# Four-layer transformer block on one core: where the input tile of the third and fourth layer begins in SBUF

## The reference

```python
def first_block(x, ...):
    for layer in range(DEPTH):                    # 2
        h = rms_norm(x, g_mix[layer])
        x = x + (even_mixer if layer == 0 else odd_mixer)(h, ...)   # attention
        h = rms_norm(x, g_mlp[layer])
        x = x + squared_relu_mlp(h, w_up[layer], w_down[layer])     # 1024 -> 4096 -> 1024
...
def mlstm_mixer(h, w_in, ...):                    # third layer
    x_in, z = jnp.split(h @ w_in, 2, axis=-1)     # 1024 -> 4096
    ...
def nsa_mixer(h, w_in, ...):                      # fourth layer
    q, k_c, v_c, k_s, v_s, k_w, v_w, z, g_logit = jnp.split(h @ w_in, ..., axis=-1)
    ...
```

## Time and profile before

| | |
|---|---|
| median of 3 runs | 935.82 us (935.81 to 936.11) |
| time of the profiled execution | 935.42 us |
| its span | 933.6 us |
| mean granted TensorE clock | 0.998 of 2.4 GHz |
| TensorE busy | 921.1 us, 99% |
| LDWEIGHTS / VectorE / ScalarE busy | 84% / 67% / 60% |

### The profile page before, as it was taken

The page is one execution under the profiler, slowest core; times in us unless marked ns, Lnnn a source line. Parts: engine busy times, 40 slices in busy tenths (PEclk is TensorE's granted clock), DMA queues, the critical chain, the costliest instruction groups (busy, mean ns, idle before and its releaser), DMA issues.

```text
span 933.6 us, 14097 instructions
## 1 busy us (share of the span) xinstructions
PE 921.1 (99%) x5584; PEld 784.7 (84%) x5584; DVE 629.9 (67%) x1137; ACT 561.8 (60%) x927; POOL 100.5 (11%) x145
## 2 busy tenths in 40 slices
PE   9999999999999999999999999999999999999997
PEld 7876888888888877788888888999988889988876
DVE  6767687764455666568776354677479847777885
ACT  6697565553435687755554343656477547868773
POOL 0210000000000000000000007155002201311101
PEclk9999999999999999999999999999999999999999
DMA  9843565555554435146555565233333642731201
GB/s 365 317 138 125 181 214 191 180 193 208 185 181 161 156 133 178 64 142 220 201 188 185 199 212 209 92 135 136 136 135 101 232 176 98 258 126 53 99 23 46
DMA packets 23017, 153.51 MB, mean 164 GB/s; under 512 B 2632, under 2 KB 2888, under 8 KB 5544
## 3 DMA queue, kind: packets, MB, share of 16 engines
q1 hardware_dynamic: 22024, 149.17, 44.5%
q0 software_dynamic: 640, 3.15, 1.0%
q10 hardware_dynamic: 288, 0.30, 0.1%
HBM read 150.57 MB, written 1.05 MB: 162 GB/s over the span
## 4 chain that ended last, share of the span: by engine, by line
PE 89%; ACT 4%; DVE 4%; issue 1%; DMA 1%; SPq 0%; ACTq 0%; DVEq 0%
PE bank L189 19%; PE bank L190 18%; PE bank L191 18%; PE bank L1165 13%; PE bank L1169 7%; PE bank L931 1%; PE bank L2334 1%; PE bank L955 1%; PE bank L944 1%; PE bank L1607 1%; PE bank L2325 1%; PE bank L2349 1%; DVE w_hi_lo L159 1%; PE bank L761 1%; PE bank L1592 1%
## 5 line engine op out<-in xcount | busy, mean ns | idle before, releaser
L159 DVE TENSOR_TENSOR w_hi_lo<-raw,w_hi_lo 128x2048 fp32r<-128x2048 f32 x121 | 277.3, 2295 | 135.4 <-ACT w_hi_lo L155 135.3
L155 ACT ACTIVATE w_hi_lo<-raw 128x2048 fp32r<-128x2048 f32 x135 | 257.8, 1912 | 107.8 <-PE bank L191 106.3
L189 PE MATMUL bank<-h,w_hi_lo 128*128 128x256 f32 x448 | 128.3, 286 | 0.2 <-DVE ml_x L1869 0.2
L190 PE MATMUL bank<-h,w_hi_lo 128*128 128x256 f32 x448 | 124.7, 278 | 0.0
L191 PE MATMUL bank<-h,w_hi_lo 128*128 128x256 f32 x448 | 124.6, 278 | 0.0
L1165 PE MATMUL bank<-h,w_hi_lo 128*128 128x512 f32 x512 | 123.1, 391 | 0.0
L1165 PEld LDWEIGHTS bank<-h,w_hi_lo 128*128 128x128 f32 x512 | 93.8, 188 | 18.3 <-issue 0.2
L189 PE MATMUL bank<-w_hi_lo,mlp_u_hi 128*128 128x512 f32 x256 | 99.8, 390 | 0.0
L190 PE MATMUL bank<-w_hi_lo,mlp_u_hi 128*128 128x512 f32 x256 | 99.6, 389 | 0.0
L191 PE MATMUL bank<-w_hi_lo,mlp_u_lo 128*128 128x512 f32 x256 | 99.6, 389 | 0.0
L190 PEld LDWEIGHTS bank<-h,w_hi_lo 128*128 128x128 f32 x448 | 84.7, 189 | 0.4 <-issue 0.2
(11 more groups left out here) (400 smaller groups left out, 1578.9 us busy)
## 6 DMA issues: line engine op xcount, KB each, us to landing
raw<-in_chunks SPq DMA_DIRECT2D x136, 1024.0 KB, 4.8
even_bias<-in_even POOLq DMA_DIRECT2D x8, 384.0 KB, 3.4
xres<-in_x SPq DMA_DIRECT2D x2, 512.0 KB, 5.4
raw<-in_chunks SPq DMA_DIRECT2D x2, 512.0 KB, 6.4
ml_z<-in_ml SPq DMA_DIRECT2D x1, 896.0 KB, 6.5
nsa_qtwo<-nsa_qraw SPq DMA_DIRECT2D x8, 80.0 KB
small<-in_small SPq DMA_DIRECT2D x1, 559.5 KB, 11.9
final_gain<-in_fnorm SPq DMA_DIRECT2D x1, 512.0 KB, 3.4
```

What stands on the lines that cost most here:

```text
L155: act.activation(w_hi[slot][:, :], raw[slot][:, :], ACT.Copy).then_inc(hi_ready, 1)
L159: dve.tensor_tensor(w_lo[slot][:, :], raw[slot][:, :], w_hi[slot][:, :].bitcast(F32), ALU.subtract).then_inc(lo_ready, 1)
L189: pe.matmul(dst, a_hi, b_hi, start=start, stop=False)
L190: pe.matmul(dst, a_hi, b_lo, start=False, stop=False)
```

## The change

The room of `h` begins 32 bytes earlier (the pad in front of it is 24 floats in place of 32) and has 8 floats more, so that everything behind it stays where it was. Within it there are now three views. `h` of the first two layers is 24 floats in, at its old address (residue 128). `h_ml` of the third layer is 16 floats in: residue 96, 32 bytes below the weights. `h_nsa` of the fourth is at the start: residue 32, 96 bytes below. Names are replaced accordingly, the writers of the tile (`Turned`) included. No instruction is added, removed or moved on any engine.

```diff
-    sb(ctx, "pad_h", [P, 32])
+    sb(ctx, "pad_h", [P, 24])
...
-    H_SHIFT = 16
+    H_SHIFT, ML_SHIFT, NSA_SHIFT = 24, 16, 0
     h_room = sb(big, "h", [P, H_SHIFT + KT * 2 * S], F32R)
-    h_moved = h_room[:, 0:KT * 2 * S].rearrange("p (k x s) -> p k x s", k=KT, x=2)
-    h = h_room[:, H_SHIFT:H_SHIFT + KT * 2 * S].rearrange("p (k x s) -> p k x s", k=KT, x=2)
+    h, h_ml, h_nsa = (h_room[:, at:at + KT * 2 * S].rearrange("p (k x s) -> p k x s", k=KT, x=2)
+                      for at in (H_SHIFT, ML_SHIFT, NSA_SHIFT))
...
-                last = product(pe, dst, w_hi[slot][:, cols], w_lo[slot][:, cols], hm_hi[:, k, :], hm_lo[:, k, :],
+                last = product(pe, dst, w_hi[slot][:, cols], w_lo[slot][:, cols], h_ml[:, k, 0, :], h_ml[:, k, 1, :],
...
-    ml_turned = Turned("mlin", sm("ml_norm"), (4, 5, 6, 7), h_moved)
+    ml_turned = Turned("mlin", sm("ml_norm"), (4, 5, 6, 7), h_ml)
...
-                last = product(pe, dst, w_hi[slot][:, cols], w_lo[slot][:, cols], hm_hi[:, k, :], hm_lo[:, k, :],
+                last = product(pe, dst, w_hi[slot][:, cols], w_lo[slot][:, cols], h_nsa[:, k, 0, :], h_nsa[:, k, 1, :],
...
-            last = wide_half(pe, c, t, bank[2 + t][:, :], hm_hi, hm_lo, range(part * WIDE_KT, (part + 1) * WIDE_KT),
+            last = wide_half(pe, c, t, bank[2 + t][:, :], h_nsa[:, :, 0, :], h_nsa[:, :, 1, :], range(part * WIDE_KT, (part + 1) * WIDE_KT),
...
-    nsa_turned = Turned("nsin", sm("nsa_norm"), (4, 5, 6, 7), h_moved)
+    nsa_turned = Turned("nsin", sm("nsa_norm"), (4, 5, 6, 7), h_nsa)
```

More of the change, by code:

```diff
@@ L1280, in build @@
     open_stages.append([])
-    H_SHIFT = 16
+    H_SHIFT, ML_SHIFT, NSA_SHIFT = 24, 16, 0
     h_room = sb(big, "h", [P, H_SHIFT + KT * 2 * S], F32R)
-    h_moved = h_room[:, 0:KT * 2 * S].rearrange("p (k x s) -> p k x s", k=KT, x=2)
-    h = h_room[:, H_SHIFT:H_SHIFT + KT * 2 * S].rearrange("p (k x s) -> p k x s", k=KT, x=2)
+    h, h_ml, h_nsa = (h_room[:, at:at + KT * 2 * S].rearrange("p (k x s) -> p k x s", k=KT, x=2)
+                      for at in (H_SHIFT, ML_SHIFT, NSA_SHIFT))
     h_hi, h_lo = h[:, :, 0, :], h[:, :, 1, :]
-    hm_hi, hm_lo = h_moved[:, :, 0, :], h_moved[:, :, 1, :]
     x_half = [sem(f"x_half{g}") for g in range(N_G)]
@@ L2280, in gates @@
                 w = slice(k * GW, (k + 1) * GW)
-                last = product(pe, bank[2][0:GW, 0:S], self.wg_hi[:, w], self.wg_lo[:, w], hm_hi[:, k, :], hm_lo[:, k, :],
+                last = product(pe, bank[2][0:GW, 0:S], self.wg_hi[:, w], self.wg_lo[:, w], h_nsa[:, k, 0, :], h_nsa[:, k, 1, :],
                                k == 0, k == KT - 1)
```

## The result

| | before | after |
|---|---|---|
| median | 935.92 us (935.81 to 936.23, 10 runs) | 938.49 us (938.22 to 938.68, 10 runs) |
| profiled execution: span | 933.6 us | 936.7 us |

The ratio is 1.0027, with a 95% interval of 1.0018 to 1.0036: the change costs 2.6 us. I had forecast no change (935.8 us, own range 934.3 to 937.4).

What follows compares the result with a forecast made beforehand. TensorE, busy in every slice at full clock, was taken as the bound, so matmul pitch decides. A kept mixture of two pitches, -1.5 to +2.1 us, gave 935.8 us, own range 934.3 to 937.4, overall range 933.2 to 939.6.

Steps and rivals of the forecast that it cites:

- the same two locks: Third and fourth layers' input matmuls: 32 and 96 below keep a mixture of 117.9 and 113.6 ns pitches, -1.5 to +2.1 us.
- a misread row: Narrow matmul groups: 16 stationary columns, taken as equal residues, record 278 ns against 276 for 48 columns at 64 below.
- the high one: Rival, third and fourth layers: 807 low-pitch matmuls go to the high pitch, 4.5 ns each, +3.6 us, 939.4 us; chance 0.20.
- the floor: Lowest pitch of a 256-column fp32r matmul, 113.3 ns or 272 cycles at 2.4 GHz; nothing expected under it.
- the right witness: `compress`, relative position not a multiple of 64 bytes: 117.9 ns per 256 columns, counted for less, having no time to lock.
- a nanosecond won or lost on a matmul of these stages is a nanosecond of the whole: Third and fourth layers' input stages: TensorE busy 132.3 of 132.9 us, 43.0 of 43.0 and 83.8 of 86.8.
- 40% were in the high one: Third and fourth layers before: mean record 278 ns, between 276 and 281, puts 40% of matmuls at the high pitch.
- the equal-residue rival: Third and fourth layers: pitch returns to 120 ns, +6.6 us for both, 942.4 us; chance 0.10 for one or both.
- The skill's rule: Moving operand and weights are read through independent ports, so no offset matters and the time is 935.8 us exactly.

Runs made afterwards that it cites:

- the maps: Three small kernels without the model's computation, run once each, traced for matmul pitch by distance below the weights: 120 ns at 0, 113.3 or 117.8 at 64, 118.3 at 32.
- e1: Kernel before with only the third layer's input moved, to 32 below (fourth stays at 64): 937.10 us against 935.80, ratio 1.0014.
- e2: Kernel before with only the fourth layer's input moved, to 96 below (third stays at 64): 937.28 us, ratio 1.0015.
- the third map: Small kernel without the computation: six input tiles against 128, 64 or 16 weight columns and weights 32 or 64 bytes higher; at input 0: 120.0, 113.3 (16 columns), 113.3 (64 higher).
- the first map: Small kernel without the computation: twenty input distances, three kinds of stretch start, some matmuls the other way round; 113.3 ns at 144 below from all three starts.
- e4: Kernel before with the third layer's input at 160 below, fourth left at 64: 937.97 us against 935.70, ratio 1.0024.
- e5: Kernel before with third and fourth layers' inputs at 0 below, the weights' own residue: 939.66 us against 935.35, ratio 1.0046.
- the fine map: Small kernel without the computation: all 64 distances in steps of 4 bytes, two stretch starts each; 117 to 124.4 ns between multiples of 16, worst at 124 below.

## Why the prediction was wrong

**The step that failed.** It is this: "So equal residues cost something at once, when both streams start in step, and a displacement takes that away. By that reading 32 and 96 below are displaced as 64 is, and are subject to the same two locks." They are displaced and not subject to the same locks. Each distance has steady pitches of its own (118.3 at 32; 117.3 and 118.7 at 96), and the two of 64, 113.3 and 117.8, belong to 64. The maps and e1, e2 show it. I had one steady displaced distance in the trace and made a class of it.

The step also rested on a misread row. I took the 16 stationary columns of `wf_hi` for a case of equal residues. Only the tile's start has residue 128: from one block k to the next its 16 columns move on by 64 bytes, and the 48 columns of `nsa_wg_hi` by 192, so that the distance changes within the group. Those matmuls of `wf_hi` start 117.0 ns apart on the mean (297.59 to 300.28 us), while 16 columns at a true distance of 0 have 113.3 ns in the third map. So that row said nothing on equal residues.

**The rival that came nearest** is the high one. Its place was right, the in tiles of both layers that had been at 113.3 ns. Its time, 939.4 us, was 0.9 too high, and that it came so near is in part luck: it took the 117.8 ns that belong to 64 below, and the steady pitches of 32 and 96 happen to lie within 1 ns of it, where the maps have 120 to 124 ns at other distances. And the mechanism that I gave it, "no longer a whole multiple of 64 bytes", is wrong: 144 reaches the floor, 128 doesn't. `compress` was the right witness, and I had discounted it for having no time to lock. That other distances don't lock at the floor was just what it showed. (Its 117.9 ns was counted a little low: between the two rows lie 31 matmuls of 256 and 32 of 128 columns, with pitches of 118.4 and 59.5 ns.)

**The sizes.** Pitches: third layer (118.25 - 115.40) x 727 = 2.1 us, fourth (117.88 - 115.30) x 546 = 1.4 us, 3.5 us in sum, near the 3.6 of the rival. What was off is the premise that "a nanosecond won or lost on a matmul of these stages is a nanosecond of the whole": the stages grew by 1.59 and 1.30 us. Part of the rest was hidden in waits. TensorE's busy share of 99% did not show the slack at the edges of stretches, since a gap of 0.44 us between two starts counts as 0.16 us of idle time when the record ahead lasts 0.28 us.

**The premises that held.** The pitch and not the busy share is what matters; no stretch had a steady pitch under the floor of 113.3 ns; there are two pitches at 64, and which one comes depends on what came ahead (the maps get both; after eight matmuls of 128 columns the first map has 113.3 and the third 117.8, so the kind of start alone doesn't decide it); 40% were in the high one (by pitches 47%, first ones included); the writers of `h` (L769 and L776, 474 to 479 ns before and after), the order and the other layers are unchanged; L1169 stays at 283 ns. The records told each layer's change, but not its size (e4). The price of the equal-residue rival, 6.6 us (its own terms add up to 6.5), was too high: e5 lost 4.3 us. And 32 below isn't half way back to it.

**The skill's rule.** At 0 and 64 below the kernel's own pitches had already spoken against it, and the third map shows the load of the weights as the other party: at input 0 the pitch is 120.0 ns with 128 stationary columns, 113.3 with 16, and 113.3 with 128 columns that lie 64 bytes higher. The Trainium skill (TensorE: Matmul & The Clock Gate, "Step-by-step: what each phase is for") has loading the next tile's weights take no read bandwidth from the running matmul. For fp32r with 256 moving and 128 stationary columns the measurements have the running matmuls pay for where those weights lie, by up to 11 ns each (124.4 at 124 below). Whether it is read bandwidth that they lose, no run shows.

**What stays open** is what in the hardware makes these pitches. The numbers say that they depend on the distance of the two tiles modulo 256, on the number of stationary columns, on which operand moves and how long it is, and at some distances on what came ahead of the stretch. Why 144 converges to the floor from any start and its neighbours 140 and 148 (121.6 and 120.0) don't, I can't say. That 256 is the period, and not more, rests on tiles at different multiples of 256 having the same pitches in all maps and in the kernel.

## What to carry to other kernels

Where matmuls of 256 fp32r columns follow each other with a new stationary tile of 128 columns each time, the distance between the two tiles' addresses is worth some 6% of the time of those matmuls (113.3 against 120.0 ns), and it takes no instruction to set. In this kernel that was 0.5% of the whole, from 934.96 us at 144 below to 939.66 at 0, and nearly all of it lies on the side of the loss. It has to be measured at each distance, for each shape and each way round: one small kernel whose trace holds a stretch for every distance, from several starts, would have foretold the direction of this change and its size within 1 us. The value at one distance says nothing of its neighbours, and a row that seems a poor witness because it never settles may be showing exactly that.

## What the runs showed of the hardware that I had not expected

- 113.3 ns for 256 columns and 226.7 for 512 is the best steady pitch of fp32r matmuls with a load of 128 columns each in all runs, 17 cycles at 2.4 GHz for 16 columns. Plain fp32 matmuls go by another measure: 128 columns at 109 ns in most of the kernel before and at 111 to 112 ns in the maps.
- Most distances (49 of 64 in the fine map) don't settle at one pitch but at a pattern of several, 113 to 129 ns. At 32 below it comes back to within 1 ns in the maps and in the kernel after.
- A step of 4 bytes can change the pitch by 7 to 8 ns (140, 144 and 148 below: 121.6, 113.3 and 120.0).
